# Orders of calls in a decoder kernel: the first microseconds, the softmax mixer, both ends of the HGRN2 stage

## The reference

```
x = LN(a*x + 0.5*FFN1(x));  x = LN(a*x + mixer(x));  x = LN(a*x + 0.5*FFN2(x))      # per layer
layer 0 mixer: h = x @ w_in;  q, k (rotary), v, u = split(h)
   o_a = rms_norm((softmax(q0 k0) - lam * softmax(q1 k1)) v)        # 4 heads, causal
   o_b = (windowed means of u - u) @ pool_w * pool_scale            # windows 2, 4, 8, 16
   y = concat(o_a, o_b) @ w_o
layer 1 mixer (HGRN2): q, f, i, g = split(x @ w_in);  8 heads, chunkwise linear recurrence with decays
   y = (rms_norm(o) * silu(g)) @ w_o
FFN(x) = (silu(x @ w_gate) * (x @ w_up)) @ w_out                    # width 2816
```

## Time and profile before

| | |
|---|---|
| Median of 3 runs | 1012.9 us (1012.82 to 1013.2) |
| The profiled execution | 1012.43 us, of it the span in the trace 1010.6 us |
| PE, share of the span | 98% |
| DVE, ACT, POOL | 71%, 50%, 3% |
| Granted PE clock, mean | 0.997 |
| Chain that ended last | PE 93%, DVE 5%, ACT 1%, issue 1% |
| Transfers | 184.27 MB, mean 182 GB/s |

### The profile page before, as it was taken

The page is one execution under the profiler, slowest core; times in us unless marked ns, Lnnn a source line. Parts: engine busy times, 40 slices in busy tenths (PEclk is TensorE's granted clock), DMA queues, the critical chain, the costliest instruction groups (busy, mean ns, idle before and its releaser), DMA issues.

```text
span 1010.6 us, 13955 instructions
## 1 busy us (share of the span) xinstructions
PE 994.7 (98%) x5126; PEld 841.2 (83%) x5126; DVE 718.1 (71%) x943; ACT 500.9 (50%) x570; POOL 34.2 (3%) x61
## 2 busy tenths in 40 slices
PE   8999999999999999999999999999999999999996
PEld 7888888887788888888888888878888888888885
DVE  5686667776779665667885657788877876666665
ACT  5673544346547553542453434457867535434330
POOL 0100000000210000000000000000001100000000
PEclk9999999999999999999999999999999999999998
DMA  9687655453656665664565656543333656656521
GB/s 293 218 269 245 208 174 200 151 208 109 224 204 214 204 206 169 212 208 139 191 228 188 194 179 197 177 133 118 103 107 98 230 173 216 212 168 211 175 98 42
DMA packets 129400, 184.27 MB, mean 182 GB/s; under 512 B 5968, under 2 KB 104928, under 8 KB 129360
## 3 DMA queue, kind: packets, MB, share of 16 engines
q1 hardware_dynamic: 126592, 174.09, 51.9%
q0 software_dynamic: 2624, 9.59, 2.7%
q10 hardware_dynamic: 144, 0.07, 0.0%
HBM read 182.67 MB, written 1.05 MB: 182 GB/s over the span
## 4 chain that ended last, share of the span: by engine, by line
PE 93%; DVE 5%; ACT 1%; issue 1%; DMA 0%; SPq 0%; DVEq 0%
PE psum L1480 24%; PE psum L1454 17%; PE psum L1456 17%; PE psum L1455 17%; PE psum L1484 12%; PE psum L1909 2%; PE psum L1895 1%; PE psum L1896 1%; DVE w_lo L821 1%; PE psum L1449 1%; PE psum L1585 1%; DVE xT L844 1%; ACT arena L567 0%; DMA raw<-in_ffn_w_in 0%; DVE stats L856 0%
## 5 line engine op out<-in xcount | busy, mean ns | idle before, releaser
L821 DVE TENSOR_TENSOR w_lo<-raw,w_hi 128x2048 fp32r<-128x2048 f32 x161 | 367.4, 2286 | 45.4 <-ACT w_hi L405 44.8
L1480 PE MATMUL psum<-xT,w_hi 128*128 128x512 f32 x1024 | 358.4, 395 | 0.0
L405 ACT CAST w_hi<-raw 128x2048 fp32r<-128x2048 f32 x161 | 304.3, 1911 | 28.2 <-DMA raw<-in_ffn_w_in 16.2
L1484 PE MATMUL psum<-xT,w_lo 128*128 128x256 f32 x1024 | 275.4, 279 | 0.0
L1480 PEld LDWEIGHTS psum<-xT,w_hi 128*128 128x128 f32 x1024 | 190.1, 188 | 41.4
L1484 PEld LDWEIGHTS psum<-xT,w_lo 128*128 128x128 f32 x1024 | 192.8, 188 | 5.5
L907 DVE TENSOR_REDUCE ffn_tok<-psum 128x256 f32<-128x512 f32 x128 | 82.4, 686 | 152.7 <-PE psum L1480 152.7
L1454 PE MATMUL psum<-w_hi,xT 128*128 128x512 f32 x448 | 178.4, 398 | 4.7 <-DVE xT L844 1.6
L1456 PE MATMUL psum<-w_hi,xT 128*128 128x512 f32 x448 | 174.8, 390 | 0.0
L1455 PE MATMUL psum<-w_lo,xT 128*128 128x512 f32 x448 | 174.5, 390 | 0.0
L435 ACT ACTIVATE ffn_tok<-ffn_tok 128x256 f32<-128x256 f32 x64 | 26.8, 418 | 229.7 <-DVE ffn_tok L907 229.5
(11 more groups left out here) (181 smaller groups left out, 712.2 us busy)
## 6 DMA issues: line engine op xcount, KB each, us to landing
raw<-in_ffn_w_in SPq DMA_DIRECT2D x170, 512.0 KB, 4.7
raw<-in_ffn_w_out SPq DMA_DIRECT2D x88, 512.0 KB, 4.0
raw<-in_c_w_in SPq DMA_DIRECT2D x32, 512.0 KB, 4.6
raw<-in_ab_w_in SPq DMA_DIRECT2D x16, 512.0 KB, 4.7
raw<-in_ab_w_o SPq DMA_DIRECT2D x8, 512.0 KB, 3.9
raw<-in_c_w_o SPq DMA_DIRECT2D x8, 512.0 KB, 4.3
raw<-in_ffn_w_in SPq DMA_DIRECT2D x12, 256.0 KB, 6.5
ln_gb<-in_ln_gain POOLq DMA_DIRECT2D x6, 512.0 KB, 5.3
```

Of the source, the lines that this page charges most:

```text
L405: nc.scalar.copy(w_hi[:, n % RING], raw[:, slot]).then_inc(hi_ready, 1)
L821: nc.vector.tensor_tensor(w_lo[:, n % RING], raw[:, n % RAW], w_hi[:, n % RING].bitcast(F32), ALU.subtract).then_inc(lo_ready, 1)
L1480: return nc.tensor.matmul(dst, w_hi[:, slot, cs], xT_both[:, kk].rearrange("p a f -> p (a f)"), start=kk == 0, stop=kk == KB - 1)
L1484: return nc.tensor.matmul(dst[:, 0:SEQ], w_lo[:, slot, cs], xT_hi[:, kk], start=False, stop=False)
```

## The change

It moves calls in the lists of PE, ACT and DVE, drops one warming matmul call, and gives oT of the C stage two banks in turn. Nothing is computed differently.

```diff
+        OT_BANK = [bank[0], bank[7], bank[0], bank[7]]
...
 ACT, mix_ab
                 exps(0)
                 exps(1)
-                wT_copy(0)
                 split_hi(s0 + AHEAD + 6)
                 u_copy(0)
+                wT_copy(0)
+                split_hi(s0 + AHEAD + 7)
+                wT_copy(1)
                 exps(2)
-                wT_copy(1)
-                split_hi(s0 + AHEAD + 7)
                 u_copy(1)
-                for b in range(2):
-                    act.wait_ge(S["dT_done"], b + 1)
-                    nc.scalar.copy(dT[:, 2 * b:2 * b + 2], bank[4 + b].rearrange("p (g f) -> p g f", g=2)
-                                   ).then_inc(S["dT_ready"], 1)
+                dT_copy(0)
                 exps(3)
+                dT_copy(1)
                 wT_copy(2)
...
 ACT, mix_c
                 head_state(7)
+                oT_split(0)
                 gates(1, 1, G[1])
-                oT_split(0)
                 head_squares(7)
                 oT_split(1)
                 head_norm(7)
+                oT_split(2)
                 split(17)
-                oT_split(2)
                 oT_split(3)
...
 DVE, mix_ab
                 maxima(2)
                 weights(2)
-                split_lo(s0 + AHEAD + 7)
                 maxima(3)
                 weights(3)
...
+                split_lo(s0 + AHEAD + 7)
                 split_lo(s0 + AHEAD + 8)
                 split_lo(s0 + AHEAD + 9)
...
 DVE, mix_c
                 split(0)
+                queries(0, 0, G[0])
+                xT_split(m, 1)
                 dve.wait_ge(x_ready, 4 * m)
                 nc.vector.tensor_copy(ln_gb[:], gam).then_inc(S["bound_ready"], 1)
                 dve.wait_ge(S["bound_ready"], 1)
-                queries(0, 0, G[0])
                 decays(0, 0)
-                xT_split(m, 1)
                 split(1)
...
                 head_scores(7, own)
+                oT_split(0)
                 head_gate(1, 0, 0, 2)
-                oT_split(0)
                 head_gate(1, 1, 0, 2)
...
 PE, program_start
                 first_xT(0, 0)
-                warm(5)
-                first_piece(0, 0, 0)
+                warm(4)
                 first_xT(1, 0)
                 warm(2)
                 for k in range(PIECES):
                     for t in range(TT):
-                        if k + t:
-                            first_piece(0, k, t)
+                        first_piece(0, k, t)
...
 PE, mix_ab
                 pe.wait_ge(S["v_ready"], 1)
-                project(s0 + 6, None, 0, G[0], FIRST)
+                project(s0 + 6, None, 0, G[0])
                 weights_T(0)
-                project(s0 + 6, None, 0, G[0], SECOND)
-                outputs(0)
-                scores(2)
                 pe.wait_ge(S["v_ready"], 2)
                 project(s0 + 6, None, 1, G[1], FIRST)
                 weights_T(1)
+                outputs(0)
+                scores(2)
                 project(s0 + 6, None, 1, G[1], SECOND)
                 scores(3)
...
 PE, mix_c
                 head_levels(7)
-                half(7, 1, SECOND)
+                project(s0 + 14, None, 1, G[1], SECOND[:2])
+                head_oT(0)
+                project(s0 + 14, None, 1, G[1], SECOND[2:])
                 u0 = s0 + 2 * len(C_CHUNKS)
-                head_oT(0)
                 head_outputs(7)
                 head_oT(1)
...
 PE, head_oT(p)
                 pe.wait_ge(S["head_gated"], 2 * p + 2)
-                if p:
-                    pe.wait_ge(S["headT_lo"], p)
+                if p == 0:
+                    pe.wait_ge(S["state_ready"], 8)
+                elif p == 1:
+                    pe.wait_ge(S["head_scores_ready"], 16)
                 else:
-                    pe.wait_ge(S["state_ready"], 8)
+                    pe.wait_ge(S["headT_lo"], p - 1)
```

More of the change, by code:

```diff
@@ L570, in exps, with dT_copy @@
                 ins.then_inc(S["probs_ready"], 1)
+            def dT_copy(b):
+                act.wait_ge(S["dT_done"], b + 1)
+                nc.scalar.copy(dT[:, 2 * b:2 * b + 2], bank[4 + b].rearrange("p (g f) -> p g f", g=2)
+                               ).then_inc(S["dT_ready"], 1)
             def u_copy(t):
@@ L780, in oT_split @@
                 act.wait_ge(S["headT_done"], p + 1)
-                nc.scalar.activation(xT_hi[:, 2 * p:2 * p + 2], bank[0].rearrange("p (h f) -> p h f", h=2), ACT.Copy,
-                                     scale=cols[:, 1:2]).then_inc(S["headT_hi"], 1)
+                nc.scalar.activation(xT_hi[:, 2 * p:2 * p + 2], OT_BANK[p].rearrange("p (h f) -> p h f", h=2),
+                                     ACT.Copy, scale=cols[:, 1:2]).then_inc(S["headT_hi"], 1)
             act.dma_start(ident[:], consts[:, C_ID:C_ID + P]).then_inc(const_landed, 16)
@@ L1341, in oT_split @@
                 dst, src = xT_lo[:, 2 * p:2 * p + 2], xT_hi[:, 2 * p:2 * p + 2]
-                nc.vector.scalar_tensor_tensor(out=dst, in0=bank[0].rearrange("p (h f) -> p h f", h=2), scalar=cols[:, 1:2], in1=src.bitcast(F32),
+                nc.vector.scalar_tensor_tensor(out=dst, in0=OT_BANK[p].rearrange("p (h f) -> p h f", h=2), scalar=cols[:, 1:2], in1=src.bitcast(F32),
                                                op0=ALU.mult, op1=ALU.subtract).then_inc(S["headT_lo"], 1)
@@ L1943, in head_oT @@
                     for t in range(TT):
-                        ins = nc.tensor.transpose(bank[0][:, (2 * h + t) * P:(2 * h + t + 1) * P],
+                        ins = nc.tensor.transpose(OT_BANK[p][:, (2 * h + t) * P:(2 * h + t + 1) * P],
                                                   o_half[hh // 4][:, t, (hh % 4) * P:(hh % 4 + 1) * P], ident[:])
```

## The result

The changed kernel takes 1008.1 us, the median of six executions (1007.78 to 1008.31); the kernel before takes 1012.88, also of six (1012.58 to 1016.59). The medians differ by 4.8 us. The ratio is 0.9945, 95% interval [0.9934, 0.9956], or 5.6 us: it lies near the ratio of the means (1013.49 and 1008.06, 5.4 us apart), and one execution of before, at 1016.59, is in them. A second set of six gave 1008.30 against 1012.74, 4.4 us, ratio 0.9952 [0.9934, 0.997]. The profiled execution took 1008.0 against 1012.43, also 4.4. The forecast of 1008.8 was 0.5 to 0.7 us high. One execution of before in the experiments took 1421.33 us at a mean granted clock of 0.655, where all others have about 0.997, and is in none of the ratios.

A forecast was written before the change was run, and what follows sets the result against it. PE, busy in 98% of the span, was taken as the bound, so time could come only from its waits. Gains of 0.6 + 0.6 + 1.8 + 1.1 = 4.1 us from 1012.9 gave 1008.8 us, range 1007.6 to 1010.7.

The forecast's parts named there:

- part 1: Program start: transposes of x's second tile ahead of the wait for w_lo; gain 0.6 us, bounds 0.3 to 0.7.
- part 2: Score part of the softmax mixer: calls reordered on PE and DVE; gain 0.6 us of the 1.7 at out_rows(0,0).
- it takes 5.1 us, so 7.0: Program start: the load of x's second tile, issued at 1.9, lands 5.1 us later, at 7.0.
- landing 4.9 us later: Mixer: the second transfer of unit s0+13's load lands 4.9 us after its issue, at 261.8.
- The late load: Mixer: load of unit s0+13 goes at 256.5 instead of 249.1; PE waits 1.1 us for oT's low half.
- the load is no obstacle: Rival in the mixer: load ready in time, part 2 gives 1.35 us, total 4.9, 1008.0; chance 0.15.
- the load turns the part into a loss: Rival in the mixer: landing takes 9.1 us, not 4.9; PE 3.6 us later than now, sum -0.1; chance 0.05.
- Part 3: HGRN2 start: PE's 1.6 us wait for xT's low half of tile 1 goes; gain 1.8 us, low bound 1.5.
- Part 4: HGRN2 end: oT(0) issued earlier, oT(1) in another bank, no PE wait; gain 1.1 us, low bound 0.8.
- The thin margin at oT(1)'s low half: HGRN2 end: due at 796.1, comes at 795.9, 0.2 us of margin; losing it is within a rival of chance 0.14.
- The clock: Rival at the start: PE's 1.4 us idle brings back half rate, 1.7 us lost, total 2.4, 1010.5; chance 0.06.
- The sum: Whole kernel: 0.6 + 0.6 + 1.8 + 1.1 = 4.1 us gained, giving 1008.8 us.

The follow-up runs named there:

- f1: Changed kernel with the w_lo subtraction of unit s0+10 put on DVE between maxima(3) and weights(3); 1007.46 us against 1012.70 of before, ratio 0.9953.
- e1: Kernel before with part 1 of the change alone (transposes of x's second tile ahead of the first piece); median 1011.66 us, ratio 0.9992.
- h1: The changed kernel run again, on one chip beside h2 and h3; median 1008.30 us, ratio 0.9952 to the kernel before.
- h2: f1 run again, on one chip beside h1 and h3; median 1007.27 us, ratio 0.9945 to the kernel before.
- f4: Changed kernel with the load of x's second tile issued one weight piece later; 1009.30 us, 1.2 us above the changed kernel.
- e2: Kernel before with part 2 of the change alone (softmax mixer); median 1012.31 us against 1012.73 of before, ratio 0.9996.
- e3: Kernel before with part 3 of the change alone (HGRN2 start); median 1010.85 us against 1012.73 of before, ratio 0.998.
- e4: Kernel before with part 4 of the change alone (HGRN2 end, two banks in turn); median 1011.78 us against 1012.73 of before, ratio 0.9992.
- f3: Changed kernel with oT of the HGRN2 stage in one bank four times, each waiting for the low half before; 1008.58 us, ratio 0.996 to before.
- g1: Changed kernel with the load of x's second tile issued ahead of the first weight piece; 1009.43 us, ratio 0.9965 to before.
- h3: Changed kernel without part 2 (score part in the orders of before); median 1008.68 us, ratio 0.9955 to the kernel before.
- g3: g2 with g1's order of loads added; 1007.92 us, ratio 0.995 to the kernel before.
- f2: Changed kernel with cast and subtraction of the late-loaded unit s0+13 put behind both halves of oT; 1009.31 us, ratio 0.9975 to before.
- g2: f1 with outputs(3) ahead of out_rows(0,0) on PE and wT_copy(3) ahead of squares(0) on ACT; 1007.71 us, ratio 0.995 to before.

## Where the prediction was right, and the terms it mis-sized

The mechanism held in all four parts. The step that failed is a term of the sum: the landing of x's second tile in part 1, for which the forecast had one time and its range no other. The landing of unit s0+13 in part 2 was mis-sized too, by less and the other way.

**Part 1: right in its chain, wrong in its size.** The failed step is "it takes 5.1 us, so 7.0". That was one execution; in the changed kernel's trace x landed at 6.41, PE waited 0.7 us for it and not 1.4, and the part brought 1.30 us instead of 0.6. The forecast allowed for no other landing; its bounds, 0.3 to 0.7, came from ACT alone. The same load, issued at 1.9, landed between 6.28 and 6.98 in the thirteen traces that have it there, and before's 6.98 was, with f1's, the latest of all; the median is 6.57. That the one sample lay at the end was bad luck. Behind the landing the 2.3 us forecast were 2.2 in every trace in which PE waits for that landing: 8.61 behind 6.41 in the changed kernel, 8.76 behind 6.57 (e1), 9.17 behind 6.98 (f1), 9.15 behind 6.95 (h1), 8.63 behind 6.43 (h2). f4 moved the landing by hand, and the matmul followed. Before, the 9.91 did not hang on this landing, so over these landings part 1 is worth 9.91 - (landing + 2.2), 0.7 to 1.4, and 1.1 at the median one; e1 measured 1.07, the changed kernel's trace 1.30. The 9.91 is one execution as well: the other three traces with the order of before have that matmul at 9.96 (e2), 10.13 (e3) and, with the half rate lasting on, 11.36 (e4).

**Part 2: 0.3 to 0.5 instead of 0.6.** The band matmuls came 0.92 us earlier within the stage (0.94 forecast), `out_rows(0,0)` 1.66 (1.7 forecast), and PE waits 1.1 us for the low half of oT, as forecast. The remaining error sits in the load: with part 1's 1.33 taken off, the forecast had the issue at 255.17 and the landing at 260.47; they came at 255.26 and 260.82. So the term "landing 4.9 us later" is short by about a quarter of a microsecond, 5.15 in the chain. Over the six traces with this order it took 4.92 (f4), 4.98 (f3), 5.01 (g1), 5.06 (h1), 5.15 (the changed kernel) and 5.18 (e2), and the AB stretch follows it: 84.96, 84.99, 85.06, 85.10, 85.18 and 85.19. So the part is worth 0.52 at a landing of 4.92, near the forecast for 4.9, and 0.29 at 5.18. By medians e2 and h3 measured it both ways, 0.42 and 0.38.

**The late load is shown, not argued.** Releasing it earlier (f1, h2) removes the wait and brings 1.0 us. The rival "the load is no obstacle" falls with it: in those six traces PE waits 0.8 to 1.1 us for oT's low half. That the load turns the part into a loss fell too: the landing was never near 9 us.

**Part 3: 1.9 instead of 1.8.** No wait is left at the second tile of xT, and all 1.86 us reach the levels of head 7 and the end. **Part 4: 1.2 by the trace, 0.95 by medians, 1.1 forecast.** The thin margin at oT(1)'s low half held: DVE has it at 792.35 (791.61 + 0.74) and PE's projection goes on at 792.47, 0.1 of the 0.2 forecast. What the forecast did not say is that most of the gain (0.8) is the order, not the bank (f3).

**The clock.** The rival needed half rate behind the idle time at the start. The changed kernel idles 0.7 us printed ahead of 6.46, and its next matmuls run at the full rate, which is the level of 2.4 GHz: they start 0.11 us apart, where the first ones of the program started 0.21 apart. After the 1.45 us of f4 too, the projection matmuls of 512 columns start at 9.07, 9.38 and 9.62, the pitch of the rest of the kernel. No run here had a longer gap ahead of those transposes. The Trainium skill, "TensorE: Matmul & The Clock Gate", section "HAM oscillation — how this bites in real kernels", warns of idle gaps between matmul bursts; up to 1.45 us, no gap here brought the half rate back. What the forecast took as fixed is when the first half rate ends, about 4.4: in e4 it lasted until 9.4 and in g3 until 8.1, and delayed PE there.

**The sum.** 4.1 forecast; 4.4 by the profile and by the second set, 4.8 by the first. In the profile the difference of 0.3 is made up of 0.7 more at the start, 0.3 less in the mixer, 0.2 more in the HGRN2 stage and 0.3 lost in the last store. That errors of both signs cancel in part is luck. The first set has 0.35 us more than the profiles, since the profiled execution of before lies 0.45 below its median and the changed kernel's 0.1.

**Open.** Why g1's executions spread, when the half rate of the start ends, and the step of 2 us told below.

## What to carry to other kernels

A background step that is moved out of the way takes along the load that its end releases. Follow that load to its consumer, and see what stands behind the consumer on the same in-order engine; the best place for such a step is where its engine waits for a partner anyway, which also keeps the release early. Moving the consumer instead only passes the wait on (f2). And a term that hangs on one DMA landing wants the landing from several executions, with its spread in the range: with one sample at the end of the spread, the term here came out at about half of what it was worth.

## What the runs showed of the hardware

The landing of one load of 256 KB at the program's start spread by 0.7 us (6.28 to 6.98 for an issue at 1.9). In the kernels with part 1 it shifted the whole kernel with it, since PE has no slack after it. Placed one transfer later in the queue (issue at 2.5) it took 5.6 us from issue to landing in its one trace (f4), not 4.4 to 5.1.

The time at which the warming matmuls get to the full rate differs from execution to execution. PE's first twelve matmuls start 0.21 us apart in all sixteen traces; the change to 0.11 comes between 4.2 us (f3, h3) and 9.4 us (e4), in both kernels at 4.4. The mean granted clock of the profile reads 1.00 there throughout, so only the pitch of the matmuls shows it. In e4 even the first projection ran at half rate: compared with the 9.91 of before the kernel lost 1.45 us, a part of which is its first x tile, which landed at 4.48 instead of 3.82.

A small operation of GpSimd is not always small. POOL's timeline of the changed kernel, the same instruction on the same 128x2 operand for different heads:

```profile
737.82 0.22 POOL L1426 TENSOR_SCALAR ssq<-ssq 128x2 f32<-128x2 f32 x1 [14.04 <-ACT psum L770]
...
767.41 2.04 POOL L1426 TENSOR_SCALAR ssq<-ssq 128x2 f32<-128x2 f32 x1 [12.86 <-ACT psum L770]
...
789.83 1.91 POOL L1426 TENSOR_SCALAR ssq<-ssq 128x2 f32<-128x2 f32 x1 [8.84 <-ACT psum L770]
```

The 2.04 (or 2.05) stands at the same head in all sixteen traces and costs nothing there. The last one takes 1.91 in every kernel with part 4 and 0.19 in every kernel without it; why is open. In g2's profiled execution, of 1009.67 where its fastest took 1007.2, the first of them was slow:

```profile
737.53 3.10 POOL L1426 TENSOR_SCALAR ssq<-ssq 128x2 f32<-128x2 f32 x1 [14.04 <-ACT psum L770]
```

and PE waited 2.0 us for what hangs on it. Single executions 1.8 to 4 us above their median are found in before, e1, f1, f2, f4, h1, h2 and h3 too; whether they are this was not seen, since they carry no profile.
